# First block of an attention layer: the second query heads' sums, norm and split moved ahead on VectorE, one squaring moved back on ScalarE

## What is computed

```python
qkv = u @ wqkv                                   # 16 query heads, 4 key heads, 4 value heads of 64
q = rmsnorm(q, gq); k = rmsnorm(k, gk)           # each head by itself
scores = einsum(q, k) * HD ** -0.5               # a block of 128 queries against 256 keys
scores = scores - slopes * dist                  # and -inf outside the window
m = maximum(scores.max(-1), sink)
e = exp(scores - m)
probs = e / (e.sum(-1) + exp(sink - m))
o = einsum(probs, v) @ wo
```

## Time and profile before

| | us |
|---|---|
| median of 3 runs | 1082.31 (1082.21 to 1082.42) |
| the profiled execution, its own time | 1081.98 |
| its span, first to last instruction | 1080.2 |
| PE busy in the span | 1066.9 (99%) |
| DVE busy | 779.6 (72%) |
| ACT busy | 477.7 (44%) |
| POOL busy | 148.7 (14%) |

### The profile page before, as it was taken

How to read it: one execution, slowest core, us unless ns; L and a number is a source line. 1 busy time by engine, 2 the same in 40 slices (tenths; PEclk the granted TensorE clock), 3 DMA queues, 4 the chain that set the end, 5 groups by cost and what they waited for, 6 DMA issues and landing times.

```text
span 1080.2 us, 14531 instructions
## 1 busy us (share of the span) xinstructions
PE 1066.9 (99%) x5014; PEld 884.4 (82%) x5014; DVE 779.6 (72%) x1147; ACT 477.7 (44%) x841; POOL 148.7 (14%) x271
## 2 busy tenths in 40 slices
PE   8999999999999999999999999999999999999998
PEld 6788888887888888888888888888888888888887
DVE  7877877778354599776677668376776878747985
ACT  7566666667323233413322342353333335427451
POOL 7544445443000000000000000000000000001000
PEclk9999999999999999999999999999999999999999
DMA  7000000050332325353343254998988898660102
GB/s 273 21 21 19 19 19 25 15 195 20 117 118 78 117 78 200 132 196 121 148 179 149 85 194 177 389 413 280 285 291 289 294 329 310 215 234 1 39 30 88
DMA packets 67232, 167.49 MB, mean 155 GB/s; under 512 B 5088, under 2 KB 6376, under 8 KB 67176
## 3 DMA queue, kind: packets, MB, share of 16 engines
q1 hardware_dynamic: 67152, 166.75, 42.9%
q10 hardware_dynamic: 24, 0.01, 0.0%
HBM read 128.99 MB, written 37.75 MB: 154 GB/s over the span
## 4 chain that ended last, share of the span: by engine, by line
PE 88%; DVE 7%; issue 2%; ACT 2%; POOL 1%; DMA 1%; SPq 0%; ACTq 0%; DVEq 0%; POOLq 0%
PE pair L2566 28%; PE pair L2546 22%; PE pair L2269 10%; PE pair L2413 8%; PE pair L2612 6%; PE pair L2504 3%; PE pair L2340 3%; PE pair L2308 2%; PE pair L2639 2%; PE pair L2474 1%; PE pair L2319 1%; POOL k_rstd L790 1%; DMA RES<-in_a_wqkv 1%; PE pair L2234 0%; DVE RES L1944 0%
## 5 line engine op out<-in xcount | busy, mean ns | idle before, releaser
L2566 PE MATMUL pair<-uT 128*128 128x512 f32 x1344 | 305.9, 389 | 0.0
L2566 PEld LDWEIGHTS pair<-uT 128*128 128x128 f32 x1344 | 252.0, 188 | 52.5 <-DVE uT L1957 0.3
L1296 ACT ACTIVATE uT<-wo_raw 128x1024 fp32r<-128x1024 f32 x83 | 84.6, 1054 | 114.0 <-PE pair L2566 97.3
L1957 DVE TENSOR_TENSOR uT<-wo_raw,uT 128x1024 fp32r<-128x1024 f32 x83 | 98.6, 1222 | 45.8 <-ACT uT L1296 45.5
L772 POOL TENSOR_SCALAR row_var<-row_ssq 128x1 f32<-128x1 f32 x16 | 3.1, 195 | 708.7 <-ACT hn L1337 625.5
L2413 PE MATMUL pair<-WA,oT 128*128 128x512 f32 x384 | 90.3, 392 | 0.6 <-DVE oT L1720 0.4
L2269 PE MATMUL pair<-WA,xT 128*128 128x512 f32 x336 | 83.7, 397 | 1.2 <-DVE xT L1516 0.4
L2413 PEld LDWEIGHTS pair<-WA,oT 128*128 128x128 f32 x384 | 71.2, 188 | 15.9 <-issue 1.4
L2546 PE MATMUL pair<-WA,WB 128*128 128x512 f32 x336 | 78.2, 389 | 0.4 <-ACT xr L1271 0.4
L2546 PEld LDWEIGHTS pair<-WA,WB 128*128 128x128 f32 x336 | 63.0, 188 | 13.8 <-DVE WB L1891 0.8
L2269 PEld LDWEIGHTS pair<-WA,xT 128*128 128x128 f32 x336 | 60.9, 188 | 14.4 <-issue 2.3
(11 more groups left out here) (239 smaller groups left out, 1790.0 us busy)
## 6 DMA issues: line engine op xcount, KB each, us to landing
wo_raw<-in_m_w SPq DMA_DIRECT2D x71, 512.0 KB, 6.4
wo_raw<-hid_kept SPq DMA_DIRECT2D x41, 512.0 KB, 5.8
hid_kept<-RES SPq DMA_DIRECT2D x32, 512.0 KB, 2.7
emb<-in_m_w SPq DMA_DIRECT2D x17, 512.0 KB, 6.1
RES<-in_m_w SPq DMA_DIRECT2D x8, 1024.0 KB, 6.8
uT_f<-in_m_w SPq DMA_DIRECT2D x6, 1024.0 KB, 6.6
RES<-in_a_wqkv SPq DMA_DIRECT2D x10, 512.0 KB, 8.6
emb<-hid_kept SPq DMA_DIRECT2D x10, 512.0 KB, 5.8
```

Source lines behind the costliest of these rows:

```text
L1296: nc.scalar.activation(operand(t, which, HI), unit(t, which), ACT.Copy).then_inc(op_hi, 1)
L1957: nc.vector.tensor_tensor(operand(t, which, LO), unit(t, which), operand(t, which, HI).bitcast(F32), ALU.subtract).then_inc(op_ready, 1)
L2566: mm = nc.tensor.matmul(ps[4 * (j % 2) + m][:], operand(t, 0, s)[:, k, m * P:(m + 1) * P], operand(t, 1, r)[:, k, :], start=(g == 0 and k ...
```

## The change

In block 0 alone:

- VectorE: `head_sums("q8")` comes ahead of `add_bias` of group 0 (before: behind it). `head_scale("q8")` and `v_diff` come right behind that `add_bias` (before: behind `invert` and `scale_probs` of group 0).
- VectorE: `q_lo_part("q8")`, both instructions, come ahead of `add_bias` of group 1 (before: behind it).
- ScalarE: `x_squares(1)` comes behind `q_hi_part("q8")` and ahead of `exps` of group 1 (before: behind `exps` of group 0, ahead of `q_hi_part`).

TensorE's, GpSimd's and SyncE's streams are the same, and no instruction is added or removed.

```diff
@@ scalar, body @@
                     if j == 1:
                         q_hi_part("q8", n, 0)
                         q_hi_part("q8", n, 1)
+                        if first:
+                            x_squares(n + 1)
...
-                    if j == 0 and not last:
+                    if j == 0 and not first and not last:
                         x_squares(n + 1)
@@ vector, body @@
                     if j == 0 and first:
                         xT_lo_half(1, 0)
                         xT_lo_half(1, 1)
+                        head_sums("q8", n)
                         add_bias(n, j, first)
-                        head_sums("q8", n)
+                        head_scale("q8", n)
+                        v_diff(n)
                         invert(n, j)
                         scale_probs(n, j)
-                        head_scale("q8", n)
-                        v_diff(n)
                         continue
+                    if j == 1 and first:
+                        q_lo_part("q8", n, 0)
+                        q_lo_part("q8", n, 1)
                     if j == 0:
                         head_sums("q8", n)
                     add_bias(n, j, first)
...
-                    if j == 1:
+                    if j == 1 and not first:
                         q_lo_part("q8", n, 0)
                         q_lo_part("q8", n, 1)
```

## The result

| | before | changed |
|---|---|---|
| median, 18 runs each | 1082.24 us (1081.59 to 1082.57) | 1084.64 us (1084.26 to 1084.93) |
| the profiled execution, its span | 1081.98, 1080.2 | 1084.64, 1082.9 |

The ratio is 1.0022, with a 95% interval from 1.0016 to 1.0028: slower, by an amount that is small but clear of the noise. The forecast was 1084.8.

A forecast was written before the change was run, and what follows sets the result against it. TensorE, busy 1066.9 of 1080.2 us, bounds the kernel. 1.28 us at group 2's scores plus 1.44 less 0.25 at the q8 projection gives +2.47, from the median 1082.31 to 1084.8 us; range 1083.4 to 1085.6.

The forecast's parts named there:

- the forecast chain: Block 0: late bias delays group 1's exponentials, q0's squares and sums, then GpSimd's queue, scaled keys and q8 projection; +2.47 us.
- the forecast's own line of 2.2 us: Smallest difference a measurement was said to tell from no change, about 0.2%; the line lay at 1084.5 us.
- its chances of 0.61 and 0.37: Forecast chances for the whole run: slower 0.61, same 0.37; faster by over 0.2% had 0.02.
- Sums ahead of group 0's bias: VectorE, block 0: the sums take 0.60 us ahead of the bias, so group 1's scores start 0.60 later, at 33.87.
- Transposes of q8: TensorE, block 0: they no longer wait for the scaled heads but for TensorE itself, starting at 37.07, 0.27 us later.
- Split ahead of group 1's bias: VectorE, block 0: the split waits for ScalarE's high part with the bias queued behind; group 2's scores 1.28 us late.
- What is late next: Into block 1: late exponentials, squares and sums delay GpSimd's root and the scaled keys; q8's projection waits 1.44 us, at 52.81.
- The squares of x at no cost, up to 1.2 us if the bias were not late: ScalarE, block 0: 1.05 us of squares fit a 2.6 us hole; without late bias they delay group 1's exponentials up to 1.2.
- The clock: TensorE's clock stays full through new waits of 1.7 and 1.44 us, no loss; rival of one fall, 1090.3 us, chance 0.02.
- The shift stays: Behind block 0 all engines are shifted alike and TensorE has no idle time to make it good; +2.47 us remains.

The follow-up runs named there:

- b1: The kernel before with only the split of q8 moved ahead of group 1's bias; 1084.51 us, ratio 1.0021.
- a3: The changed kernel with GpSimd's norm of block 1's keys ahead of the third group's bias tiles; 1083.45 us, ratio 1.0011.
- a1: The changed kernel with the split of q8 put back behind group 1's bias; 1083.14 us, ratio 1.0009.
- a2: The changed kernel with the split of q8 and the squares of x both put back; 1082.00 us, ratio 0.9999.
- b3: The kernel before with only the sums of q8 moved ahead of group 0's bias; 1082.97 us, shift +0.42.
- b4: The kernel before with the difference of values put behind q8's split instead of ahead of group 1's bias; 1082.42 us, ratio 0.9999.
- d1: b4 with GpSimd's bias tiles of groups 0 and 1 later and the keys' norm ahead of the third group's tiles; 1082.43 us, ratio 1.0.

## Why the prediction was right

Step by step, with the changed kernel's distances, the forecast chain is in the trace at every step, and the shift that it adds up to (2.47) was measured as 2.43 by the traces and 2.40 by the medians. The measured shift passes the forecast's own line of 2.2 us by 0.2 only, so that "slower" and not "same" was close, as its chances of 0.61 and 0.37 said.

- *Sums ahead of group 0's bias*: 0.60 forecast for group 1's scores, 0.60 measured (3.76 against 3.16).
- *Transposes of q8*: 0.27 late forecast, 0.16 measured. The term was 1.05 + 2.15 from rows of other places; here the eight scores and nine matmuls took 1.02 and 2.07 (33.80, 34.82, 36.89). The wait for qn went and the lost 0.6 ate it, as said.
- *Split ahead of group 1's bias*: +1.28 forecast for group 2's scores, +1.22 measured; the 0.06 are 0.11 from the transposes and 0.07 from the high part (0.63 behind them instead of 0.70), less 0.12 because the bias work followed the split without an overlap (39.81 against 38.24 + 1.53). So part of the agreement is two small errors of opposite sign. The releaser is rmax. b1 shows that this is the part that costs.
- *What is late next*: the q8 projection +2.47 forecast, +2.43 measured, its wait of 1.44 (from a natural start 0.42 behind the transposes) measured as 52.70 - 50.81 - 0.42 = 1.47. a3 shows that this wait is GpSimd's queue, by taking 1.23 us away without touching group 2's scores. The forecast followed the delay into that queue by the exponentials, squares and sums alone, and left out GpSimd's own wait for group 1's bias additions. That the number did not suffer is luck: the two ways end 0.03 us apart, at 44.61 and 44.64.
- *The squares of x at no cost, up to 1.2 us if the bias were not late*: both halves hold; a1 against a2 gives 1.14 by the medians, 1.02 by the traces. The later load of x held nothing up either: from the q8 projection to the transposes of x TensorE took 8.81 us (52.70 to 61.51), before 8.79 (50.34 to 59.13).
- *The clock*: the granted clock is full in all slices of the changed kernel, through waits of 1.56 and 1.29 us. The rule of the Trainium skill (TensorE: Matmul & The Clock Gate, "Part 1: The HAM clock gate") that idle time brings the throttled clock back took no effect in these waits; no run here shows how long a wait would have to be.
- *The shift stays*: from block 1 on nothing is made good. In every kernel of the table the shift of the median is within 0.13 us of the shift at block 1's q8 projection.

Two of the expectations behind it were mis-sized. b3's 0.6 left out that in the kernel before the scale stood 0.80 behind the scaled probabilities, since it waited for GpSimd's root. With the early sums it follows 0.61 behind, and gives 0.19 of the 0.60 back. b4's 0.33 took the bias work as 1.63 us wherever it stands.

## What to carry to other kernels

Where an engine runs a fixed order, an instruction moved ahead brings its own wait with it. Ask what the engine could have done in that wait: here 1.63 us of bias work that was ready would have fitted into the wait of 1.77 us for the high part, and the bias, not the split, was what the next scores waited for last. Then follow the delay through every in-order queue that it enters, by every wait by which it can enter, until one has slack; half of the loss came from a GpSimd queue two steps on, where reordering one norm won it back.

## What the runs showed of the hardware that was not expected

The bias work of group 1 took 0.24 us longer in b4 than in the kernel before (1.87 against the 1.63 of the earlier trace rows, 36.99 to 38.62), and 0.22 longer in d1 (1.85). In both its first addition was followed by its accumulator read after 0.38 us instead of some 0.21. In both only the two predicated copies stood between the scaled heads and that addition; in the kernel before the values' difference stood there too. Moving GpSimd's tiles away did not change it. Small operations of GpSimd (37.42 in b4, 37.51 in d1) and the start of ScalarE's high part (37.40, 37.81) fall beside that addition as well, and no run takes them away. The cause stays open.

Handovers between engines were steady enough to forecast by: from the end of VectorE's nmax to ScalarE's exponentials 0.03 to 0.04 us, from the start of nmax to TensorE's next scores 0.11, in the kernel before (33.16 to 33.27) and in the changed one (33.69 to 33.80, 41.44 to 41.55). From the end of the scaled keys to TensorE's q8 projection it was 0.15 in the changed kernel (52.55 to 52.70), as in the kernel before.
